# Block 2's scores of units 0 to 31: from fp32 products of 64 rows to fp32r products of high and low parts

## The reference

```python
q_rot = _partial_rope(q, pos)                 # 8 heads in 2 groups of 4, d = 64
k_s_rot, k_w_rot = ...                        # one key of 64 dims for each of 2 groups, per branch
ss = einsum('bghqd,bgqnkd->bghqnk', q_rot, k_s_rot) * scale      # "sel"
sw = einsum('bghqd,bgkd->bghqk', q_rot, k_w_rot) * scale         # "win"
p = softmax(where(mask, s, -1e30));  o = p @ v
o = g0 * o_cmp + g1 * o_sel + g2 * o_win
```

## Time and profile before

| | |
|---|---|
| median of 3 runs | 1713.03 us (1711.38 to 1713.83) |
| the profiled execution | 1705.67 us |
| its span | 1703.7 us |
| mean granted clock of TensorE | 0.993 |
| TensorE busy | 1647.6 us (97% of the span) |
| VectorE, ScalarE, GpSimd busy | 1114.0, 714.2, 576.8 us |
| units 0 to 31 of layer 0 and of layer 1 | from 510.36 and from 1183.14 us of the span |

### The profile page before, as it was taken

How to read it: one execution, slowest core, us unless ns; L and a number is a source line. 1 busy time by engine, 2 the same in 40 slices (tenths; PEclk the granted TensorE clock), 3 DMA queues, 4 the chain that set the end, 5 groups by cost and what they waited for, 6 DMA issues and landing times.

```text
span 1703.7 us, 25404 instructions
## 1 busy us (share of the span) xinstructions
PE 1647.6 (97%) x9563; PEld 1280.2 (75%) x9563; DVE 1114.0 (65%) x1955; ACT 714.2 (42%) x1426; POOL 576.8 (34%) x594
## 2 busy tenths in 40 slices
PE   7988999999999999999999999999999999999997
PEld 4455547478785668888888878887667888888886
DVE  6999756345237665777778654533774587777854
ACT  4233342243226654444444334233664454444322
POOL 1010001231205563544445624110564454444460
PEclk9999999999999999999999999999999999999999
DMA  6314230045211003333333313622000333333321
GB/s 195 69 25 94 56 123 1 22 117 173 76 50 51 2 1 100 95 102 101 100 100 100 95 45 112 185 63 99 2 2 1 99 112 100 99 100 101 100 98 50
DMA packets 195019, 136.91 MB, mean 80 GB/s; under 512 B 34487, under 2 KB 176562, under 8 KB 194898
## 3 DMA queue, kind: packets, MB, share of 16 engines
q1 hardware_dynamic: 188604, 128.07, 25.7%
q10 hardware_dynamic: 6294, 7.22, 1.8%
HBM read 131.00 MB, written 2.10 MB: 78 GB/s over the span
## 4 chain that ended last, share of the span: by engine, by line
PE 78%; DVE 12%; POOL 4%; issue 2%; DMA 2%; ACT 2%; ACTq 0%; POOLq 0%; DVEq 0%; SPq 0%
PE ps L563 14%; PE ps L564 14%; PE ps L565 14%; PE ps L2119 4%; PE ps L2120 4%; PE ps L2121 4%; PE ps L1999 4%; PE ps L2015 4%; PE ps L2030 3%; PE ps L1199 3%; POOL U_LO L2712 1%; DMA WR<-in_cmp_w_v 1%; PE ps L1107 1%; PE ps L605 1%; PE ps L1887 1%
## 5 line engine op out<-in xcount | busy, mean ns | idle before, releaser
L565 PE MATMUL ps<-HT_R,WR_R 128*128 128x512 f32 (+1 forms) x832 | 313.1, 376 | 0.0
L565 PEld LDWEIGHTS ps<-HT_R,WR_R 128*128 128x128 f32 x832 | 156.8, 189 | 31.7
L563 PE MATMUL ps<-HT_R,UP_HI 128*128 128x512 f32 x448 | 177.3, 396 | 0.0
L564 PE MATMUL ps<-HL_MLP,UP_HI 128*128 128x512 f32 x448 | 177.0, 395 | 0.0
L485 DVE TENSOR_TENSOR WR_R<-WR,UP_HI 128x1024 fp32r<-128x1024 f32 x56 | 100.0, 1785 | 103.1 <-ACT UP_HI L479 103.1
L2191 ACT ACTIVATE BIG<-ps 64x512 f32<-64x512 f32 (+3 forms) x124 | 71.7, 580 | 180.4 <-PE ps L565 161.0
L2516 DVE CUSTOM_DVE_ANT_0 ps<-ps,tri 128x512 f32<-128x512 f32 (+1 forms) x192 | 93.1, 503 | 58.6 <-PE ps L1999 57.9
L2686 POOL TENSOR_SCALAR BIG<-BIG,rg,gate 128x512 f32<-128x512 f32 (+3 forms) x128 | 76.6, 611 | 151.9 <-DVE rg L2532 151.6
L2291 ACT ACTIVATE BIG<-ps,mn 128x512 f32<-128x512 f32 (+1 forms) x192 | 100.3, 528 | 60.9 <-DVE mn L2516 53.9
L2712 POOL TENSOR_TENSOR U_LO<-BIG,U_HI 128x768 fp32r<-128x768 f32 (+1 forms) x48 | 120.5, 2531 | 1.9
L893 PE MATMUL ps<-WR,HT 128*128 128x512 f32 (+1 forms) x256 | 112.7, 590 | 1.2 <-ACT BIG L1676 1.2
(11 more groups left out here) (398 smaller groups left out, 4279.1 us busy)
## 6 DMA issues: line engine op xcount, KB each, us to landing
WR<-in_w_up SPq DMA_DIRECT2D x64, 512.0 KB, 4.0
WR<-in_w_down SPq DMA_DIRECT2D x96, 256.0 KB, 3.2
WR<-in_w_in SPq DMA_DIRECT2D x36, 512.0 KB, 5.4
WR<-in_w_out SPq DMA_DIRECT2D x6, 2048.0 KB, 7.8
WR<-in_w_in SPq DMA_DIRECT2D x5, 2048.0 KB, 8.4
WR<-in_w_down SPq DMA_DIRECT2D x16, 512.0 KB, 3.7
WR<-in_cmp_w_k SPq DMA_DIRECT2D x2, 2048.0 KB, 8.8
WR<-in_cmp_w_v SPq DMA_DIRECT2D x2, 2048.0 KB, 8.3
```

The costliest lines, as they stand in the source:

```text
L563: nc.tensor.matmul(out_, w[0], x[0], start=start, stop=False)
L564: nc.tensor.matmul(out_, w[0], x[1], start=False, stop=False)
L565: return nc.tensor.matmul(out_, w[1], x[0], start=False, stop=stop)
```

## The change

The scores of units 0 to 31 are computed in fp32r from high parts (rounded to fp32r) and low parts (the rest), over the same keys. Two key tiles per branch are written: `K_HI` holds each group's rounded key twice, in both halves of the partitions, and `K_LO` holds its rest in partitions 64 to 127. `Q_HL` has one tile per head, with the head's low part in partitions 0 to 63 and its high part in 64 to 127. The product of `Q_HL` with `K_HI` over 128 rows sums low x high and high x high; a second product over partitions 64 to 127 adds high x low. A unit's products are at least 256 columns wide. The rotated keys are written once each, to `kraw`; ScalarE makes the high parts (`k_hi`, `q_hi`) and VectorE the low parts (`k_lo`, `q_lo`). The new tiles lie over `ksT` and `kwT`, over `qT`, over parts of `qrT` that have been read, over the forget gate's tiles, over `hidr` and over `postg`, and so the load of `postg` goes to unit 36. The waits in `q_hi` and at every eighth unit's scores guard this.

```diff
+        K_HI = [parts(f"K_HI{i}", at_BIG + 4 * (4096 + 1024 * i), 2, SEQ) for i in range(2)]
+        K_LO = [parts(f"K_LO{i}", at, SEQ) for i, at in enumerate((at_ff, at_ff + 2048, at_ff + 4096, at_hidr))]
+        Q_HL = [parts(f"Q_HL{i}", at, SEQ) for i, at in enumerate([at_BIG + 2048 * n for n in (0, 1, 2, 3, 4, 5, 6)] + [at_postg])]
...
+                if u < 4 * NH:
+                    if u % 8 == 0:
+                        pe.wait_ge(sem.score_lo, score_parts(l) + 3 + u // 8)
+                    m, n, tok = ("sel", "win").index(kind), max(P * (t + 1), 256), slice(P * t, P * t + P)
+                    for o in range(2):
+                        if u >= 2:
+                            pe.wait_ge(sem.s_exp, NU * l + 2 * (u - 2) + o + 1)
+                        nc.tensor.matmul(s_bank(u, o)[:, 0:n], Q_HL[2 * j + o][:, tok], K_HI[m][:, j // 2, 0:n], start=True, stop=False)
+                    for o in range(2):
+                        nc.tensor.matmul(s_bank(u, o)[:, 0:n], Q_HL[2 * j + o][HD:P, tok], K_LO[2 * m + j // 2][HD:P, 0:n],
+                                         start=False, stop=True).then_inc(sem.s_ps, 1)
+                    return
...
-            post_gain(w0, a["g_post_mix_2"][l:l + 1, :])
...
+            def k_hi(m):
+
+                act.wait_ge(sem.rot, NPM * l + m + 1)
+                for g in range(KVG):
+                    for o in range(2):
+                        last = copy(K_HI[m][HD * o:HD * o + HD, g, :], kraw[HD * g:HD * g + HD, m, :])
+                last.then_inc(sem.score_hi, 1)
+
+            def q_hi(j):
+
+                if j == 0:
+                    act.wait_ge(sem.rot, NPM * (l + 1))
+                    act.wait_ge(sem.cs_ps, T * (l + 1))
+                if j >= 2:
+                    act.wait_ge(sem.score_lo, score_parts(l) + 2 + j)
+                if j == 3:
+                    act.wait_ge(sem.post_y, 8 * w0)
+                copy(Q_HL[2 * j][0:HD, :], qrT[0:HD, j, :])
+                copy(Q_HL[2 * j][HD:P, :], qrT[0:HD, j, :])
+                copy(Q_HL[2 * j + 1][HD:P, :], qrT[HD:P, j, :]).then_inc(sem.score_hi, 1)
...
+            k_hi(0)
...
+                if j == 11:
+                    k_hi(1)
...
+                if n in (20, 21, 23):
+                    q_hi((20, 21, 23).index(n))
...
+                if u == 4:
+                    q_hi(3)
+                if u == 36:
+                    act.wait_ge(sem.s_ps, NU * l + 4 * NH * 2)
+                    post_gain(w0, a["g_post_mix_2"][l:l + 1, :])
...
                 if m < 2:
-                    dst = (ksT, kwT)[m]
-                    for g in range(KVG):
-                        for o in range(2):
-                            a_, b_ = slice(HD * g, HD * g + HD), slice(HD * o, HD * o + HD)
-                            last = nc.vector.tensor_tensor(dst[b_, g, :], rcos[a_, m % 2, :], rsin[a_, m % 2, :], ALU.add)
+                    last = nc.vector.tensor_tensor(kraw[:, m, :], rcos[:, m % 2, :], rsin[:, m % 2, :], ALU.add)
                 else:
                     last = nc.vector.tensor_tensor(qrT[:, m - 2, :], rcos[:, m % 2, :], rsin[:, m % 2, :], ALU.add)
                 last.then_inc(sem.rot, 1)
...
+            def k_lo(m):
+
+                dve.wait_ge(sem.score_hi, score_parts(l) + m + 1)
+                for g in range(KVG):
+                    mine = slice(HD * g, HD * g + HD)
+                    last = nc.vector.tensor_tensor(K_LO[2 * m + g][HD:P, :], kraw[mine, m, :], K_HI[m][mine, g, :].bitcast(F32), ALU.subtract)
+                last.then_inc(sem.score_lo, 1)
+
+            def q_lo(j):
+
+                even, odd = Q_HL[2 * j], Q_HL[2 * j + 1]
+                dve.wait_ge(sem.score_hi, score_parts(l) + 3 + j)
+                nc.vector.tensor_tensor(even[0:HD, :], qrT[0:HD, j, :], even[0:HD, :].bitcast(F32), ALU.subtract)
+                nc.vector.tensor_tensor(odd[0:HD, :], qrT[HD:P, j, :], odd[HD:P, :].bitcast(F32), ALU.subtract).then_inc(sem.score_lo, 1)
...
+            k_lo(0)
...
+            k_lo(1)
...
+                if t >= 4:
+                    q_lo(t - 4)
...
+                if u in (2, 8):
+                    q_lo(2 if u == 2 else 3)
...
```

More of the change, by code:

```diff
@@ L241, in build @@
         kcBD, vBD = sb("kcBD", KVG, 2, 32), sb("vBD", KVG, 4, HD)
-        hidk, hidv, hidr = sb("hidk", 2, 64), sb("hidv", 2, KVG, 32), sb("hidr", 2, KVG, 4, 32)
+        hidk, hidv = sb("hidk", 2, 64), sb("hidv", 2, KVG, 32)
+        at_hidr = nc.sbuf_base
+        hidr = sb("hidr", 2, KVG, 4, 32)
         gf, gx, gate = sb("gf", T, 32), sb("gx", T, NGATE), sb("gate", T, NGATE)
@@ L1808, in build, with score_parts @@
         PAIRS = [(kind, j) for j in range(NH // 2) for kind in ("sel", "win")] + [("fox", j) for j in range(NH // 2)]
+        def score_parts(l):
+            return (3 * H1 + 1 if first else 0) + 6 * l
         def group_of(u):
```

## The result

The changed kernel takes 1735.16 us (median of 4 runs, 1724.1 to 1737.82) against 1712.2 us: ratio 1.0131, 95% interval 1.0094 to 1.0168. The interval leaves 1 out, so the change makes the kernel slower, by 1.3%. Forecast: 1733 us. The profiled execution took 1735.28 us, with a span of 1733.5 us.

What follows compares the result with a forecast made beforehand. TensorE, busy throughout the steady score loop, was taken to bound the kernel. 16.4 us of longer score units plus 3.4 us of start and fringe made 19.8, added to the 1713.03 us median: 1733 us, range 1721 to 1744.

Steps and rivals of the forecast that it cites:

- The step of 1.17 us per four units: TensorE's score loop: four units' distances from scores to turn grow from 2.97 to 4.14 us; 14 times, 16.4 us.
- The trip itself: Each new unit's change to 64-row products and back costs TensorE 0.30 us.
- fp32r streams twice as fast per product: Score products: faster fp32r against two heads run at once before, so streaming comes out even at 512, 384 and 256.
- Rival A: Old heads' fp32 products ran one after the other, old four units 4.7 us; change faster, 1704 us; chance 0.02.
- Rival B: The trip to 64 rows is free in the score loop; 1716 us, or 1713 with a free start; chance 0.06.
- Rival C: Second 64-row score product can't load weights under the first; 11.2 us more, 1744 us; chance 0.09.
- The first exponential: Start of each layer's loop: three query copies on ScalarE, 1.8 us less a 0.65 us gap, delay it 1.15 us.
- The first turn: Start of each layer's loop: late with the first exponential by 1.15 us, plus 0.25 for VectorE's subtractions.
- the 3.4 us of this term: Start and fringe of the loop: 1.15 + 0.25 + 0.3 = 1.7 us per layer, for two layers.
- rival D: Loop start: longer wait brings another reduced-clock stretch, queries 2 and 3 may not hide; up to 4 us per layer, 1741; chance 0.05.

Runs made afterwards that it cites:

- experiment 1: Changed kernel with each head's second product reading all 128 rows (high queries against low keys left out), so no form change inside a unit; ratio 1.0041.
- Experiment 4: Changed kernel with head 0's 64-row product moved to partitions 0 to 63 (low queries, high keys), head 1's kept in 64 to 127; ratio 1.0069.
- experiment 2: Changed kernel with each head's 64-row product directly after its own 128-row one, two trips to 64 rows per unit; 1772.8 us, ratio 1.0388.
- Experiment 5: Changed kernel with the third and fourth query pairs' high parts copied at units 4 and 8, low parts at 6 and 12; ratio 1.011.

## Why the prediction was right

**TensorE's price.** The step of 1.17 us per four units measured 9.70 - 8.53 = 1.17, and 7.07 us over six fours in every layer. Experiments 1 and 4 show what its causes are worth, each alone and not as terms of one sum: taking the trip to 64 rows away gave back 1.31 us a period, letting the two 64-row products share the array 0.63. The trip itself was mis-sized by a little, 0.33 us in place of 0.30. One sentence of the forecast misreads its rows, though the sum doesn't use it: "fp32r streams twice as fast per product" holds for one record, 0.23 us against 0.43 (half of the 0.85 worked out there), and an fp32 product has two records. Rival A (the old heads ran one after the other) is excluded by the kernel before itself, whose records of the two heads start at 535.03 and 535.04, and by the time, which rose. Experiment 4 shows the same of fp32r: 64-row products in different halves start within 0.01 us of each other. Rival B (a free trip) is excluded by experiment 1. The Trainium skill (TensorEngine Tiling (Array Packing), Key Properties) says that a change of mode drains the engine, and the runs agree that it has a price: 0.33 to 0.39 us a round trip.

**Rival C** (the second 64-row product can't load its weights under the first): the pair at 512 runs from 530.10 to 530.76, 0.66 us. In experiment 2 a single 64-row product holds the array for 0.43 us (539.50 to 539.92), so the second one in the same half adds 0.23, its streaming and no more. Its weight load, one of some 0.19 us in the trace, was hidden. The Trainium skill (TensorE: Matmul & The Clock Gate, Part 3: Packing small matmuls) has a line by which it would be exposed in the same row group; the trace doesn't bear that line out.

**The other engines.** Everything ahead of the loops was hidden: the first scores come no later than before. The first exponential came 1.14 us later in the span, and the forecast said 1.15, but so close a hit is luck: the three copies took 1.91 us and not 1.8, and what was ahead of them ended 0.16 us earlier, so the gap before the exponential grew by 1.30. The first turn was later by 2.5 us and not by 1.4. The rest isn't VectorE's, for which the turn didn't wait, but mostly TensorE's own: it did units 2 and 3 at half clock. Experiment 5 restored the start and gained 2.0 us, for both layers, so of the 3.4 us of this term about 2 are shown to be the queries' place. The rest wasn't tried apart.

**The sum.** 19.8 us forecast, 19.2 at equal clock. The medians differ by 23 us in the result, because the changed kernel's executions had a lower mean clock. In the profiles the first eight units of a layer took 4.4 us more on average (20.6 against 16.2), where the forecast has 1.17 + 1.7 = 2.9. They hold 8.5 us at half clock on average against 3.4. This is rival D's mechanism, to which I gave 0.05 as a case of its own and nothing in the sum; with few profiles it isn't shown to be the change's. What remains may be the stretch at the compression products, which both kernels have in some executions; what decides in which ones stays open. That the median of the changed kernel came within 2.2 us of the forecast is in part luck: its four executions span 13.7 us.

## What to carry to other kernels

Before fp32 products are replaced by fp32r ones, look at whether the old ones share the array. Here two heads side by side in fp32 streamed for 0.85 us at 512 columns, by the estimate from the earlier trace rows, and the four fp32r products that replaced them one after another took about as long, 4 x 0.23. Of the versions run here that compute the whole decomposition, only those that keep all products in the heads' halves got down to the kernel before or below it. Count the forms of the array in a loop's round: a round trip cost TensorE 0.33 to 0.39 us here, in a loop in which it is never idle.

And when executions of one kernel differ by 1% through the clock, compare at equal clock: a difference of 0.2% was out of reach of the ratio and plain on the line. Look at the clock as well, because such a comparison hides what the change does to it.

## What the hardware showed beyond this

TensorE fell to half clock for 13.7 to 17.1 us while it was busy without a gap to speak of, with products of 62 columns behind a wait of 0.47 us in one case and 0.60 in another; the same code behind waits of 0.50 and 0.58 us ran at full clock in the first profile of the kernel before. One such stretch costs 6 to 8 us. And an fp32r product of 128 columns took 0.035 us less than one of 256 columns, so filling up to 256 gave nothing.
